# Casts held to PE's pace, norm sums held until their squares are due, and output-projection inputs in idle weight slots, in a two-layer hybrid trunk

## What is computed

```python
h = h + 0.5 * g1 * swiglu(mod(rmsnorm(h)), ffn1)          # width 2816
P = mod(rmsnorm(h)) @ w_in                                # u, v | q, k, v
h = h + g2 * (concat(sgu(u, v), dilated(q, k, v)) @ w_out)
h = h + 0.5 * g3 * swiglu(mod(rmsnorm(h)), ffn2)
```

## Time and profile before

| | us |
|---|---|
| three runs | 6022.75, 5596.76, 6031.96 |
| median of them | 6022.75 |
| the profiled execution | 5576.07 |
| its span, slowest core (4) | 5574.5 |
| spans of the eight cores | 5437.0 to 5574.5 |
| PE busy in it | 4982.6 (89%) |
| DVE, ACT, POOL busy | 2307.2, 1894.5, 662.1 |

### The profile page before, as it was taken

One profiled execution on the slowest core, in us unless ns is written; L12 is line 12 of the kernel. 1 busy time (PEld: TensorE's weight loads), 2 busy tenths in 40 slices (PEclk: granted clock), 3 DMA queues, 4 the chain that ended last, 5 costly groups with the idle time before them and its releaser, 6 DMA issues.

```text
span 5574.5 us, 83651 instructions; the slowest of 8 cores (5437.0 to 5574.5 us)
## 1 busy us (share of the span) xinstructions
PE 4982.6 (89%) x27302; PEld 2331.5 (42%) x27826; DVE 2307.2 (41%) x4066; ACT 1894.5 (34%) x2879; POOL 662.1 (12%) x701
## 2 busy tenths in 40 slices
PE   6879787799797999799989998799988899999998
PEld 2434333344343444344444443344443344444443
DVE  2323353434454544243323333544435544534442
ACT  2202242544333544122121312435534344523321
POOL 1110240000230000000010002401004100000000
PEclk9999898999898999899999999999999999999999
DMA  9898655653557473678589624535354736557331
GB/s 170 172 209 200 168 123 118 151 151 107 174 130 217 124 198 110 200 191 204 129 201 177 213 100 134 131 117 176 97 165 139 228 101 191 161 175 245 118 105 60
DMA packets 421208, 875.31 MB, mean 157 GB/s; under 512 B 154768, under 2 KB 187920, under 8 KB 414608
## 3 DMA queue, kind: packets, MB, share of 16 engines
q1 hardware_dynamic: 315760, 613.10, 35.4%
q0 software_dynamic: 40512, 139.35, 16.2%
q10 hardware_dynamic: 64512, 117.47, 6.6%
HBM read 821.94 MB, written 239.08 MB: 190 GB/s over the span
## 4 chain that ended last, share of the span: by engine, by line
PE 67%; DMA 14%; ACT 5%; issue 5%; DVE 4%; POOL 3%; SPq 2%; DVEq 0%; ACTq 0%; POOLq 0%
PE ps L719 38%; PE ps L765 17%; PE ps L926 3%; PE ps L1186 3%; DMA arena<-xP 2%; PE ps L1307 2%; PE ps L1157 2%; DMA arena<-hS 2%; DMA hS<-arena 2%; POOL arena L1007 2%; DMA kS<-arena 2%; PE ps L614 1%; DMA arena<-wgu 1%; DVE arena L997 1%; DMA arena<-ada_w 1%
## 5 line engine op out<-in xcount | busy, mean ns | idle before, releaser
L719 PE MATMUL ps<-arena 128*128 128x512 bf16 x10962 | 2534.5, 382 | 57.5 <-DMA arena<-wguS 11.0
L719 PEld LDWEIGHTS ps<-arena 128*128 128x128 bf16 x11264 | 1068.5, 98 | 1271.4 <-issue 76.2
L765 PE MATMUL ps<-arena 128*128 128x512 bf16 x5498 | 1280.3, 386 | 67.9 <-DMA arena<-wdS 30.9
L727 DVE SCALAR_TENSOR_TENSOR arena<-arena,ps 128x512 f32<-128x512 f32 x704 | 483.1, 686 | 1090.1 <-ACT arena L724 1044.2
L724 ACT ACTIVATE arena<-ps 128x512 f32<-128x512 f32 x704 | 419.5, 597 | 1448.1 <-PE ps L719 1236.5
L765 PEld LDWEIGHTS ps<-arena 128*128 128x128 bf16 x5632 | 545.7, 99 | 704.6 <-issue 101.7
L729 DVE TENSOR_TENSOR arena<-ps,arena 128x512 bf16<-128x512 f32 x704 | 487.2, 692 | 333.6 <-PE ps L719 288.7
L926 PE MATMUL ps<-arena 128*128 128x512 bf16 x2525 | 590.6, 390 | 31.9 <-DVE arena L997 25.8
L778 DVE SCALAR_TENSOR_TENSOR arena<-ps,arena 128x512 f32<-128x512 f32 x256 | 192.2, 751 | 959.7 <-PE ps L765 650.9
L1164 ACT ACTIVATE arena<-ps 128x1024 bf16<-128x1024 f32 (+1 forms) x384 | 357.9, 932 | 431.4 <-PE ps L1157 373.7
L1219 POOL TENSOR_TENSOR arena<-arena 64x512 bf16<-64x512 f32 x128 | 162.5, 1269 | 2150.8 <-ACT arena L1215 2121.6
(11 more groups left out here) (67 smaller groups left out, 2064.8 us busy)
## 6 DMA issues: line engine op xcount, KB each, us to landing
arena<-wguS SPq DMA_DIRECT2D x308, 512.0 KB, 3.9
arena<-hS SPq DMA_DIRECT2D x192, 512.0 KB, 6.8
arena<-wdS SPq DMA_DIRECT2D x112, 704.0 KB, 5.9
hS<-arena ACTq DMA_DIRECT2D x224, 256.0 KB, 6.0
arena<-hS ACTq DMA_DIRECT2D x160, 256.0 KB, 6.2
wguS<-wgu POOLq DMA_DIRECT2D x66, 512.0 KB, 16.6
hS<-arena SPq DMA_DIRECT2D x128, 256.0 KB, 8.7
arena<-ada_w POOLq DMA_DIRECT2D x120, 256.0 KB, 8.3
```

The costliest lines, as they stand in the source:

```text
L719: Sx.op("pe", lambda e, kc=kc, half=half, bk=bk: e.matmul(bank(bk), lhsT=gu[:, half, kc, :], rhs=y[:, kc, :], start=(kc == 0), stop=(kc == ...
L727: Sx.op("dve", lambda e: e.scalar_tensor_tensor(out=sg, in0=sg, scalar=1.0, in1=bank(G), op0=ALU.add, op1=ALU.mult), reads=[psB[G]], write ...
L765: Sx.op("pe", lambda e, j=j: e.matmul(bank(bk), lhsT=wd[:, j, :], rhs=act[:, j, :], start=(j == 0), stop=(j == FC - 1)), reads=[bwd, ba[j] ...
```

## The change

Seven parts, all in the order and the waits; no product is added or left out.

1. DMAs with `pace=True` (all casts of `conv_gen`, `win_cast` and `wout_cast`) also wait for the last PE product recorded before them. `wout_cast` becomes a generator; `conv_gen` has two semaphores more and larger costs per transfer.
2. `norm_steps` can wait `lead` after the load; it squares a pair only when the model finds the load 1 us old, and issues sums only when it finds the later square of the pair 0.6 us old. The ring of squares has 6 buffers for 4.
3. The mixer tiles of the first output projection lie in four of the six gate slots, and the gate loads of the next group stop at two until `open_gu`.
4. `attn_gen` waits 20 us of PE work after its first loads. The loads for the second output projection follow the attention in one generator.
5. Projection buffers: 6 for q and k instead of 4, 4 for v instead of 3; v is stored from ACT's queue; twelve small DVE steps of the Newton iteration become six.
6. `norm_steps` of the next group starts one gate block sooner (FC - 6).
7. The conditioning columns of layer 1 go at 5.8 us each instead of 8.

```diff
@@ class Sched
-    def ok(self, *bufs):
+    def ok(self, *bufs, by=0.0):
...
-        return all(self.when(b.w) <= self.t["pe"] for b in bufs)
+        return all(self.when(b.w) + by <= self.t["pe"] for b in bufs)
...
         deps = self._deps(reads, writes, accw, extra)
+        if pace and self.cnt["pe"]:
+            _merge(deps, ("e", "pe", self.cnt["pe"]))
@@ class Weights
-                if n >= self.gu_stop:
+                if n >= min(self.gu_stop, self.used_gu + NGU):
                     return
...
+            def open_gu(self, n):
+                self.gu_stop = n
+                while self.ngu < min(n, self.used_gu + NGU):
+                    self.load_gu()
@@ buffers
-        sqr = za.ring(4, [128, T], BF16, "sq")
+        sqr = za.ring(6, [128, T], BF16, "sq")
@@ conv_gen (win_cast and wout_cast get pace=True in the same way)
-                                     writes=[bWG[l, w, j]], extra=[toks[i % 4]], ns=5000.0)
+                                     writes=[bWG[l, w, j]], extra=[toks[i % 4]], ns=5000.0, pace=True)
@@ norm_steps
+            if lead:
+                yield lead
             pend = []
+
+            def mms(n):
+                while pend and pend[0][0] < n:
+                    norm_mm(*pend.pop(0))
+
             for q in range(4):
-                while not Sx.ok(*hbuf[1][2 * q:2 * q + 2]):
+                while not Sx.ok(*hbuf[1][2 * q:2 * q + 2], by=1000.0):
                     yield 500.0
-                pend.append(norm_sq(2 * q, eng=eng))
-                pend.append(norm_sq(2 * q + 1, eng=eng))
+                for kc in (2 * q, 2 * q + 1):
+                    pend.append((kc, norm_sq(kc, eng=eng)))
+                yield cost
                 if q:
-                    while q == 1 and not Sx.free(psB[NB]):
+                    while not (Sx.free(psB[NB]) or q > 1) or not Sx.ok(pend[1][1][1], by=600.0):
                         yield 500.0
-                    norm_mm(2 * q - 2, pend[2 * q - 2])
-                    norm_mm(2 * q - 1, pend[2 * q - 1])
-                yield cost
-            norm_mm(6, pend[6])
-            norm_mm(7, pend[7])
+                    mms(2 * q)
+            while not Sx.ok(pend[1][1][1], by=600.0):
+                yield 500.0
+            mms(KC)
             norm_rstd()
@@ ffn_group
-                if j == FC - 5:
+                if j == FC - 6:
...
-                        sn_ = mix.add(seq(*[norm_steps(2400.0, yv[ym[s]], *p, gate=(lambda s=s: left[s] == 0))
+                        sn_ = mix.add(seq(*[norm_steps(2400.0, yv[ym[s]], *p, gate=(lambda s=s: left[s] == 0), lead=14000.0)
@@ proj_tile
-                    n = mx.nqk % 4
+                    n = mx.nqk % 6
...
-                Sx.dma("sp", "va%d" % n, lambda e: e.dma_start(
+                Sx.dma("act", "va%d" % n, lambda e: e.dma_start(
@@ attn_gen
             nrm = iter(())
+            yield 11000.0
+            yield 9000.0
@@ project, more=False, behind its second tile
-                        w, m0 = OX(), mx.z.tile([128, KC, T], BF16, 1, "mx")
...
-                        wout_cast(l, w.w)
-                        w.mx = [m0]
+                        side["wo"] = mix.add(wout_cast(l, w.w))
+                        s0 = W.gu_stop % NGU
+                        assert s0 + 4 <= NGU and W.ngu == W.gu_stop
+                        zg = Zone(gu_lo + s0 * 4096, gu_lo + (s0 + 4) * 4096)
+                        w.mx = [zg.tile([128, KC, T], BF16, 1, "mx") for _ in range(2)]
                         load_mx(w, 0, 0)
                     if not more and k == 2:
+                        load_mx(w, 1, 2)
                         norm_load(0, hS, bHS)
@@ the layer loop
-                side["cv2"] = mix.add(conv_gen(l, 1, 24000.0))
+                side["cv2"] = mix.add(conv_gen(l, 1, 31000.0))
...
-                side["cv2"] = mix.add(conv_gen(l, 1, 14500.0))
+                side["cv2"] = mix.add(conv_gen(l, 1, 24000.0))
...
+            W.gu_stop = (8 * l + 4) * FC + 2
             ffn_group(l, 0, (6, 7), src, bsrc, FB4, posts=posts, hook=mid1)
...
-            ox.mx.append(z.tile([128, KC, T], BF16, 1, "mx"))
-            load_mx(ox, 1, 2)
-            ox.h = z.ring(8, [128, T], F32, "oh")
-            side["at"] = mix.add(attn_gen(1, 2100.0))
+            ox.h = z.ring(10, [128, T], F32, "oh")
+            side["at"] = attn_gen(1, 2000.0)
+            at1 = mix.add(side["at"])
             outproj(l, [0, 2, 1, 3], ox, FB4)
+            mix.drain(side["cv2"])
+            W.open_gu(FC * 16)
...
-                side["wo"] = mix.add(wout_again(l, ox.w, 4500.0))
+                yield from wout_again(l, ox.w, 3500.0)
                 load_mx(ox, 0, 4)
+                yield 6000.0
                 load_mx(ox, 1, 6)
...
+            at1[0] = seq(side["at"], prep2())
-                side["ada"] = mix.add(ada_gen(B0, list(range(72, 144)), 8000.0))
+                side["ada"] = mix.add(ada_gen(B0, list(range(72, 144)), 5800.0))
```

More of the change, by code:

```diff
@@ L580, in conv_gen @@
             for j in range(FC):
-                toks[i % 4] = Sx.dma("pool", "cv%d" % (i % 4), lambda e, j=j: e.dma_start(out=wguS[l, w, j], in_=wgu_d[l, w, j]),
-                                     writes=[bWG[l, w, j]], extra=[toks[i % 4]], ns=5000.0)
+                toks[i % 4] = Sx.dma("pool", "cv%d" % (i % 4 if j > 1 else j + 4), lambda e, j=j: e.dma_start(out=wguS[l, w, j], in_=wgu_d[l, w, j]),
+                                     writes=[bWG[l, w, j]], extra=[toks[i % 4]], ns=5000.0, pace=True)
                 i += 1
@@ L797, in ffn_group @@
                     for s in range(2):
-                        for q in range(4):
+                        for q in range(2):
                             Sx.dma("sp", "k%d%d%d" % (g % 2, s, q), lambda e, q=q, s=s: e.dma_start(
-                                out=keep[s][0][:, 2 * q:2 * q + 2], in_=src[tiles[s], :, 2 * q:2 * q + 2]),
-                                reads=bsrc[tiles[s]][2 * q:2 * q + 2], writes=keep[s][1][2 * q:2 * q + 2])
-                if j == FC - 5:
+                                out=keep[s][0][:, 4 * q:4 * q + 4], in_=src[tiles[s], :, 4 * q:4 * q + 4]),
+                                reads=bsrc[tiles[s]][4 * q:4 * q + 4], writes=keep[s][1][4 * q:4 * q + 4], ns=3500.0)
+                if j == FC - 6:
                     if nxt:
@@ L859, in inner @@
                 self.ntr = self.nqk = self.nva = 0
-                for v in range(3):
+                for v in range(4):
                     ap, b = self.va[v]
@@ L1017, in vapart @@
                 bk = chunk(16, True, s)
-                n = mx.nva % 3
+                n = mx.nva % 4
                 mx.nva += 1
@@ L1466, in mid1 @@
                 nonlocal mx
-                if p == "gate" and k == 14:
-                    mix.drain(side["cv2"])
                 if p == "down" and k == 4:
@@ L1476, in mid1 @@
                     side["win"] = mix.add(win_again(l, mx, 2200.0))
-            posts = seq(*[norm_steps(2200.0, (lambda k=k: mx.y2[k]), *p2(4 + k), gate=lambda: side["late"]) for k in (0, 1)])
+            posts = seq(*[norm_steps(2200.0, (lambda k=k: mx.y2[k]), *p2(4 + k), gate=lambda: side["late"], lead=14000.0)
+                          for k in (0, 1)])
+            W.gu_stop = (8 * l + 4) * FC + 2
             ffn_group(l, 0, (6, 7), src, bsrc, FB4, posts=posts, hook=mid1)
```

42 lines of the change are left out of this document (24 added, 18 removed).

## The result

The changed kernel is faster: 0.956 of the time before, 95% interval 0.945 to 0.967. The profiled execution took 5319.02 us against 5576.07, 257 us less where 310 were forecast; 5266 would have been 0.944, just under the interval. Besides the seven parts that were named, the changed kernel no longer finishes all casts of the second FFN at gate block 14 of tiles 6 and 7, and it loads a kept residual tile in two transfers instead of four. The text calls the kernels "before" and "changed".

What follows compares the result with a forecast made beforehand. PE bounds the kernel and only its waits can be won. Terms 145 - 34 + 58 + 26 + 36 + 22 + 12 + 45 = 310 us, from 5576 to 5266; range 5180 to 5430, the forecast's own 5190 to 5350.

Steps and rivals of the forecast that it cites:

- Sums, 145: Norm sums on PE: issued later behind their loads, their 199 us of waits fall to 54; 145 us won (80 to 182).
- ends, −34: End of both first projections: eight sums at one go wait for POOL's squares and modulated pairs; 17 us lost at each.
- 12 for leftovers of long waits: Norm sums: 12 us of the 54 us kept as waits, left over from long waits that shrink.
- Only half of the distance helps: Norm sums: lower bound of 80 us won, since the loads move too.
- kS, 58: QK of attention: paced casts let kS stores land sooner; 10 of 68.1 us stay, 58 won (30 to 68).
- wguS and ada_w, 26: Waits on wguS (11.0) and ada_w (15.6), laid to a burst and an unfinished loop; 26 us won (10 to 27).
- rule of turns per packet: DMA engines alternate queues per packet, so one cast slows SP like four; some 69 of 84 us would come.
- Gate ring, 36: First output projection: mS's tile lacked memory until the projection ended; gate slots let it load sooner, 36 us won (20 to 38).
- wdS, 22: Wait of 30.9 us on wdS, from SP standing before mS loads; chaining loads behind attention wins 22 us (10 to 31).
- rival 1: Casts spread into stretches that had none meet loads PE waits for: 154 us lost, 5420 us; chance 0.17.
- Small things, 12: More q/k buffers, v stores on ACT's queue, fewer DVE steps, larger residual ring: 12 us won (0 to 30).
- the clock, 45: PE loses clock after waits; some 25 of 47 long waits go and 2 come: 45 us won (20 to 110).

Runs made afterwards that it cites:

- norms alone: Kernel before with only the new norm generator (later sums, margins, lead, larger ring, start one gate block sooner); one run, 5424.54 us.
- the old norms: Kernel before with only the casts' wait for PE's newest product added, its norm generator kept; 0.983 (0.955 to 1.011) of before.
- moving one load: Changed kernel with SP's refill of the first input slot (mS, third tile) put back behind the attention's first loads; 5318.51 and 5322.16 us.
- the run with casts held: Changed kernel, no second-FFN weight casts begun in two down stages (tiles 6 and 7; 2 and 3), closer together elsewhere; 0.949 (0.939 to 0.958) of before.
- later residual rows: Changed kernel, w_in back at one block in 2.8 us, not 2.2, and first ten residual rows loaded when the output projection begins; 5319.6 us.
- the transfers themselves were spread: Changed kernel, attention begun after the output projection is issued, vS rows loaded one set at a time, 1.7 us a step; 5299.9 to 5311.9 us.

## Why the prediction was off by a sixth

The direction and the two largest mechanisms, the later sums and the casts in front of kS, were right; the forecast's own range held the time, and no rival came at its size. Two steps failed: the memory to which the wait on mS was laid, and the wait on wdS, whose stretches got new traffic that had no term. The terms, in its order:

- **Sums, 145, and ends, −34.** Net 111 forecast, 103 measured, by other parts. The ends cost 5.6 and 6.1 us before the sums and some 1.7 behind them, not 17 each: all eight squares were still to be done, as forecast, but the sums run beside them, and the gate products that were to cover 3.4 us of the modulated pairs took 5.9. With norms alone, layer 1 shows what a late load makes of the place: 26.8 us. On the other side, "12 for leftovers of long waits" was short by the output projections, 15.6 + 16.5 + 10.1 us, and the start kept 23.5 us, not 17: the first wait of 16.5 us is not among the 47, so the sum counted some of it as short waits to be won. "Only half of the distance helps" did not come. (For 155.6 of 156 us the row has 155.22 us and 710 recorded products; eight products in 1.89 us, the last 0.38, give 0.216, so the 0.2155 stands.)
- **kS, 58: 68. wguS and ada_w, 26: 27.** Right in size: 95 us came of 84. The clause "holding POOL costs nothing I can see" held, also with the old norms (78.9 us beside 78.5). By the rule of turns per packet that was weighed (Trainium skill, "DMA: Bandwidth & Descriptors", Queues, rings and completion order) 69 of the 84 us would have come. The runs do not refute the rule: norms alone had 46 of the 68 us on kS, and the conditioning columns came from part 7.
- **Gate ring, 36: 38 in its group, and nothing in the time.** This is the first step that failed. "Come from a tile that had no memory until the projection was over" was read from the code; the load PE waited for was a refill with its memory free, behind vS on SP. Undoing the ring brought no wait back; moving one load did. And the step named nothing that is late next: of 38 us, 32 came back before the sums, and 29 of these left again when the one load was moved back.
- **wdS, 22: −4, and −21 for residual rows behind DVE, which had no term.** The second step that failed, and with 47 us the largest shortfall; the whole is 53 short. The forecast laid wdS to SP standing before mS loads. The trace of before has SP and POOL at that place so, and PE in the changed kernel at another:

```profile
2282.15 1.99 POOL L581 DMA_DIRECT2D wguS<-wgu  x4
2282.76 28.96 SPq L1293 DMA_DIRECT2D arena<-hS  x9
2313.46 1.07 SPq L1281 DMA_DIRECT2D arena<-mS  x1
...
2513.55 6.19 PE L733 MATMUL ps<-arena 128*128 128x512 bf16 x16 [11.71 <-DVE arena L792]
```

  SP stood at the residual rows (L1293), beside a burst of four casts, and not at mS. In that stretch, the down stage of tiles 2 and 3, the wait did fall, from 11.7 + 13.8 to 13.3 us. What came instead is in two other stretches. In tiles 6 and 7 (11.9 on wdS, 8.4 behind DVE) it is the casts, now spread into a stretch that had none, as the run with casts held shows. That is rival 1 on a small scale: some 12 us of wait, not 154. The 11.7 us at 2513.55 stand behind the down stage of tiles 4 and 5 of the second FFN, where the conditioning columns of part 7 run faster than before; from 2470 to 2515 us SP's queue took 37.3% of the DMA engines, POOL's 31.2% and ACT's 26.3%. No run took part 7 back, so that cause is open. What is left in tiles 2 and 3 is laid to SP's own loads, since held casts changed it little (12.2) and later residual rows more (8.2).
- **Start, 0: −13** (wd 35.9 from 26.3). The experiments read 30 to 40 there, with one part alone on the kernel before 38.0 and 30.8, so part of it is the spread of executions; the rest was not tried.
- **Small things, 12, and the clock, 45.** The groups of the small things fell by 25, of which their own undoing returned 5. Short waits and clock together gave 46 us, where 12 + 45 and some 23 of short sums were forecast; most likely the clock was too large, but these rows don't part the two. The sign of a clock of 0.975 or more was just missed (0.974).

## What to carry over

Before a wait is put down to memory, look at what its load stood behind on the issuing queue: the row of the queue before the load says it, the code doesn't. When a wait of a load is taken away on a queue that is full, name the next load on that queue and who needs it, and price that; here four versions that differ in which load stands last took 5318 to 5339 us, until the transfers themselves were spread (5299.9 to 5311.9). Of two parts that cure the same wait, only runs of each alone show what they share.

## What was not expected of the hardware

SP can stand without any semaphore to wait for. In the output projection one issue of vS took 10.57 us; issues on SP mostly take 0.3 to 0.6. The DMA queues of the stretch, 1545 to 1580 us of the changed kernel:

```profile
DMA packets 11460, 9.61 MB, mean 275 GB/s; under 512 B 9219, under 2 KB 9475, under 8 KB 11201
...
q1 hardware_dynamic: 11457, 9.58, 98.2%
```

11457 packets of SP's queue fill 98.2% of 16 engines (the middle number of the last line is MB), with 9219 of all packets under 512 bytes (a row of vS is 192 numbers of two bytes, 384 bytes): 0.05 us a packet in the mean. Their number has a price: another full stretch, 2130 to 2166 us, moved 344 GB/s in 5130 packets, 275 here. That SP stands because the engines are full is likely, since it stands where they are, but no row names what it waits for. The second: the eight sums at the end of a projection take 0.58 us each where a lone product takes 0.38 elsewhere, with waits of 0.41 between them. The granted clock is 1.00 from 765 to 771 us and 0.50 (1.2 GHz) from 771.5 to 779, behind one wait of 2.75 us and seven of 0.41.
